# Second block's query, key and gate projections as seven block products of weight pairs, head norms with narrow sums

## The reference, cut to what matters

```python
hn = rms_norm(x, norm1_g[l])
proj = hn @ w_in[l]                      # 1024 x 5120
# qa, ka, va, qb, kb, vb: 8 heads of 64 each; gate_a, gate_b: 1024 wide each
out_a = chunked_attention(qa, ka, va, q_norm_g[l], k_norm_g[l], rel_bias[l])
out_b = stick_breaking_attention(qb, kb, vb)
mixed = (jax.nn.sigmoid(gate_a) * (out_a @ w_branch_a[l])
         + jax.nn.sigmoid(gate_b) * (out_b @ w_branch_b[l]))
x = x + mixed @ w_out[l]
```

## Time and profile before

| what | us |
| --- | --- |
| median of 3 runs (range) | 3571.55 (3569.49 to 3575.08) |
| the profiled execution, device time | 3567.36 |
| its span, first to last instruction | 3565.5 |
| PE busy | 3283.7 (92%) |
| DVE / ACT / POOL busy | 2166.0 / 1244.7 / 866.0 |
| mean granted clock of PE | 0.960 of full |

### The profile page before, as it was taken

How to read it: one execution, slowest core, us unless ns; L and a number is a source line. 1 busy time by engine, 2 the same in 40 slices (tenths; PEclk the granted TensorE clock), 3 DMA queues, 4 the chain that set the end, 5 groups by cost and what they waited for, 6 DMA issues and landing times.

```text
span 3565.5 us, 36894 instructions
## 1 busy us (share of the span) xinstructions
PE 3283.7 (92%) x14740; PEld 2553.0 (72%) x14740; DVE 2166.0 (61%) x2476; ACT 1244.7 (35%) x1843; POOL 866.0 (24%) x815
## 2 busy tenths in 40 slices
PE   6878998998798899999997999999889979999999
PEld 3657776666676678888886778865447767888787
DVE  5454445886676887775446571137763589888433
ACT  3332111554223433333334222137551344444322
POOL 1310210123333243331000100001653244333101
PEclk9889998999999999999999999999999999999999
DMA  3443344002344222225432434321104422222543
GB/s 141 142 148 112 106 173 148 21 22 72 129 136 137 94 95 83 83 76 175 130 123 94 142 123 121 95 73 54 36 20 142 154 71 89 83 77 77 191 128 124
DMA packets 107043, 377.98 MB, mean 106 GB/s; under 512 B 13783, under 2 KB 16471, under 8 KB 106488
## 3 DMA queue, kind: packets, MB, share of 16 engines
q1 hardware_dynamic: 61976, 217.79, 19.3%
q0 software_dynamic: 44896, 157.84, 12.5%
HBM read 296.93 MB, written 78.64 MB: 105 GB/s over the span
## 4 chain that ended last, share of the span: by engine, by line
PE 56%; DVE 10%; issue 6%; POOL 2%; ACT 2%; DMA 0%; POOLq 0%; DVEq 0%; ACTq 0%
PE PS L360 17%; PE PS L362 17%; PE PS L361 17%; DVE HL L317 1%; PE PS L2809 1%; DVE E L2941 1%; PE PS L2770 1%; PE PS L2792 1%; POOL Sc L3010 1%; DVE QR L1395 1%; DVE HTf L1665 0%; ACT HL L301 0%; DVE Rk L2621 0%; POOL HT L1831 0%; PE PS L2546 0%
## 5 line engine op out<-in xcount | busy, mean ns | idle before, releaser
L360 PE MATMUL PS<-H,HL 128*128 128x512 f32 x2176 | 874.3, 402 | 77.4 <-DVE HL L317 23.5
L362 PE MATMUL PS<-H,HL 128*128 128x512 f32 x2176 | 858.9, 395 | 0.0
L361 PE MATMUL PS<-H,HL 128*128 128x512 f32 x2176 | 857.6, 394 | 0.0
L317 DVE TENSOR_TENSOR HL<-RAW,HL 128x1024 fp32r<-128x1024 f32 (+1 forms) x412 | 480.9, 1168 | 617.1 <-ACT HL L301 612.9
L301 ACT ACTIVATE HL<-RAW 128x1024 fp32r<-128x1024 f32 (+1 forms) x412 | 368.8, 896 | 1203.6 <-PE PS L362 1111.2
L360 PEld LDWEIGHTS PS<-H,HL 128*128 128x128 f32 x2176 | 415.1, 191 | 182.0 <-DVE HL L317 32.9
L361 PEld LDWEIGHTS PS<-H,HL 128*128 128x128 f32 x2176 | 415.9, 191 | 91.6 <-issue 4.6
L362 PEld LDWEIGHTS PS<-H,HL 128*128 128x128 f32 x2176 | 414.9, 191 | 91.5
L360 PE MATMUL PS<-hsr,HL 128*128 128x512 f32 x704 | 278.4, 396 | 1.8 <-DVE rows L2096 1.8
L361 PE MATMUL PS<-hsr,HL 128*128 128x512 f32 x704 | 278.5, 396 | 0.0
L362 PE MATMUL PS<-hsr,HL 128*128 128x512 f32 x704 | 276.5, 393 | 0.0
(11 more groups left out here) (352 smaller groups left out, 5256.4 us busy)
## 6 DMA issues: line engine op xcount, KB each, us to landing
RAW<-in_w_up SPq DMA_DIRECT2D x98, 512.0 KB, 3.6
RAW<-in_w_down SPq DMA_DIRECT2D x88, 512.0 KB, 3.6
RAW<-in_w_proj SPq DMA_DIRECT2D x48, 512.0 KB, 4.3
scr_hid<-hidr POOLq DMA_DIRECT2D x36, 512.0 KB, 2.9
HTf<-scr_hid POOLq DMA_DIRECT2D x72, 256.0 KB, 3.7
RAW<-in_w_wmodr SPq DMA_DIRECT2D x32, 512.0 KB, 4.5
RAW<-in_w_wout SPq DMA_DIRECT2D x26, 512.0 KB, 3.8
RAW<-in_w_wmod SPq DMA_DIRECT2D x16, 512.0 KB, 4.1
```

Of the source, the lines that this page charges most:

```text
L317: e.tensor_tensor(lo, part_source(k, j, x)[0], hi.bitcast(F32), ALU.subtract).then_inc(*k.low.mark(j, x))
L360: e.matmul(out, lh, rh, start=first, stop=False)
L361: e.matmul(out, lh, rl, start=False, stop=False)
L362: return e.matmul(out, ll, rh, start=False, stop=last)
```

## The change

- **Projection.** The 32 units are run as 16 pairs, `P2`, normed pairs alternating with plain ones at first, each pair as seven products of 12 matrix instructions, in the feed-forward's scheme. The combinations t1 to t4 of H are formed by DVE and ACT during the values of half 1 (t1 after them, since it takes the place of a part of H). Values of half 1 now follow directly on those of half 0.
- **Middle.** The rows of half 1 are formed earlier (during value units 5 to 7 of half 0), in place instead of in a buffer `ot`; therefore the residual x is first stored to memory (`mid_store`), reloaded during the gate pairs, multiplied by its norm on DVE, and stored again.
- **Head norms.** Squares of a pair go to a tile `sqt`; 16 products of 128 tokens with columns of a selector `sel` (32 columns wide) leave the sums of the pair's 4 heads x 8 token blocks in 32 rows of 128. DVE and ACT work on these 32x128; the result is stored to memory (512 bytes a row) and read back four times 64-fold into `sqt`, which spreads each factor over its head's 64 rows; DVE then multiplies.
- **End.** The bias table and the first keys, values and queries lie where t2 to t4 lie now, so POOL loads them after m7 of the last pair, and the bias of heads 5 to 7 after its m4.

```diff
-    units("proj2", [*range(32, 40), *range(3), *range(32, 40), *range(3, 32)])
+    for _ in range(2):
+        units("proj2", range(32, 40))
+    for a, b in P2:
+        out.extend([("proj2", a, "first"), ("proj2", b, "full")])
...
+P2 = [(0, 1), (8, 9), (2, 3), (10, 11), (4, 5), (12, 13), (6, 7), (14, 15)] + [(n, n + 1) for n in range(16, 32, 2)]
...
-            if h == 0 and vs == 1 and u_ == 1:
+            if h == 0 and vs == 1 and u_ == 0:
                 free = mid_sum(k, e, F, free, 1)
...
@@ pe_proj2
+    def square_sums(i):
...
+        for a, n in enumerate(P2[i]):
+            e.wait_ge(*s.act.at("sq", n))
+            for t in range(8):
+                c = 8 * a + t
+                x = e.matmul(PS[0:32, 2, 0:128], k.sel[:, blk(c, 32)], k.sqt[:, a, blk(t)], start=c == 0, stop=c == 15)
...
+    free = pe_values(k, e, F, 0, free)
     free = pe_values(k, e, F, 1, free)
+    for i, (n0, n1) in enumerate(P2):
...
+        for x in PRODUCTS["full"]:
+            w, f, b = take_part(k, e, j, x), FACTOR[x], p2_bank(x, i)
+            claim(b)
+            for q in range(4):
+                e.wait_ge(*mid_block_ready(k, f, q))
+                hi, lo = block(k, f, q)
+                y = mm3(e, PS[:, b, :], w[0][:, blk(q)], w[1][:, blk(q)], hi, lo, q == 0, q == 3)
...
+            if normed(i - 1) and x == "m6":
+                square_sums(i - 1)
...
@@ pool_proj2
+    def load_factors(i):
+        e.wait_ge(*k.st_rq.at(i))
+        for a in range(2):
+            e.wait_ge(*s.pe.at("sq", i))
+            for hh in range(2):
+                to = k.sqt[64 * hh:64 * hh + 64, a, :].rearrange("p (t n) -> p t n", t=8)
+                c = 16 * a + hh
+                e.dma_start(to, k.d_rq[i // 2][c:c + 15:2].partition_broadcast(64)).then_inc(*k.in_rq[a].mark(i, hh))
...
+    e.wait_ge(*s.pe.at("m7", NP2 - 1))
+    load_queries(k, e, 0)
+    load_pair(k, e, 0)
+    e.dma_start(k.B[:, 0:5, :], k.A["bias2"][0:5].rearrange("h p n -> p h n")).then_inc(*k.in_bias[0].mark(0))
+    load_queries(k, e, 1)
+    load_pair(k, e, 1)
+    e.wait_ge(*s.pe.at("m4", NP2 - 1))
+    e.dma_start(k.B[:, 5:8, :], k.A["bias2"][5:8].rearrange("h p n -> p h n")).then_inc(*k.in_bias[1].mark(5))
+    e.wait_ge(*s.dve.at("x", 7, 1))
+    e.dma_start(k.d_x[7], k.xs[:, 1, :]).then_inc(*k.st_xs[1].mark(7))
+    store(NP2 - 1)
```

More of the change, by code:

```diff
@@ L2248, in pool_down @@
     for m in range(N_HALF, len(LOADED)):
+        if m == len(LOADED) // 2 + N_HALF and not F.second:
+            mid_store(k, e, F, 0)
         load_hidden(k, e, F, m)
-    if F.second:
+    if not F.second:
+        mid_store(k, e, F, 1)
+    else:
         for hf in range(2):
@@ L2490, in pool_mid_residual @@
[L2490 to L2494, removed]
[L2500 to L2506 removed]
+            mid_rows(k, e, 0, 1)
@@ L2538, in claim @@
             e.wait_ge(*x)
[L2540 to L2568, removed]
[L2569 to L2574 removed]
+    def square_sums(i):
+        e.wait_ge(*s.dve.at("sel", 2))
+        claim(2)
+        for a, n in enumerate(P2[i]):
[3 more added lines that the diff above has]
+                x = e.matmul(PS[0:32, 2, 0:128], k.sel[:, blk(c, 32)], k.sqt[:, a, blk(t)], start=c == 0, stop=c == 15)
+        x.then_inc(*s.pe.mark("sq", i))
+        free[2] = [s.dve.at("m", i)]
@@ new lines, in act_proj2 @@
+    for i in range(NP2):
+        if i:
+            finish(i - 1)
+        e.wait_ge(*s.pe.at("m1", i))
+        if i:
+            e.wait_ge(*s.dve.at("c11", i - 1))
+        e.activation(k.s1p[:, :], k.PS[:, p2_bank("m1", i), :], ACT.Copy).then_inc(*s.act.mark("s1", i))
+        by(i, "m1")
+        by(i, "m6")
+        by(i, "m5")
+        if normed(i - 1):
+            e.wait_ge(*s.dve.at("m", i - 1))
+            e.activation(k.rq[:, :], k.rq[:, :], ACT.Sqrt).then_inc(*s.act.mark("m", i - 1))
+        by(i, "m7")
+        by(i, "m2")
+        by(i, "m3")
+        by(i, "m4")
@@ new lines, in pool_proj2 @@
+    for i in range(NP2):
+        if i and not normed(i - 1):
+            store(i - 1)
+        if normed(i - 1):
+            e.wait_ge(*s.dve.at("inv", i - 1))
+            e.dma_start(k.d_rq[i // 2], k.rq[:, :]).then_inc(*k.st_rq.mark(i - 1))
+        for m in residual_rows(i - 1):
+            e.wait_ge(*s.dve.at("x", m, 1))
+            e.dma_start(k.d_x[m], k.xs[:, m % 2, :]).then_inc(*k.st_xs[m % 2].mark(m))
+            if m + 2 < 8:
+                load_x(m + 2)
+        if i + 2 < NP2:
+            pair_sums(k, e, p2_unit(k, i + 2))
+        if normed(i - 1):
+            load_factors(i - 1)
+        if normed(i - 2):
+            store(i - 2)
+        if i == NP2 - 8:
+            for n in P2[6]:
+                e.wait_ge(*s.dve.at("n", n))
+            for h in range(2):
+                e.wait_ge(*k.st_res[h].at(k.mid, 7))
+            load_x(0)
+            load_x(1)
@@ L3169, in pool_program @@
     pool_branch(k, e)
-    after(e, *k.branch.every())
+    after(e, *k.branch.every(), *k.st_xs)
     pool_halves(k, e, k.O2)
```

350 lines of the change are left out of this document (231 added, 119 removed).

## The result

The changed kernel takes **3523.8 us** (median of 4 runs, 3520.8 to 3529.0) against 3570.5 for the kernel before in runs beside it (4 runs, 3562.3 to 3575.1): a ratio of 0.9873, 95% interval 0.985 to 0.9896. The same kernel measured again later gave 3527.7 and 0.9891 (0.9877 to 0.9904). The forecast was 3526, in a range of 3511 to 3544.

The account below looks back on a forecast made before the run. PE, busy 92% of the span, was taken as the bound. Terms -39.1 - 9.7 - 6.3 + 2.0 + 0 + 7.4 = -45.7 us took the profiled 3567.36 to 3521.7; with 4.2 for the median, 3526 us, range 3511 to 3544.

Parts of the forecast that it names:

- Pairs: Projection: 16 pairs of 84 instructions at 19.32 us replace 32 units of 48 at 10.88 us; -39.1 us.
- First hole: PE's 13.23 us hole before half 1's values: rows start earlier, about 3.5 us of hole left; -9.7 us.
- Second hole: PE's 4.61 us wait for a weight split behind two head-norm inverses disappears, with its slow start; -6.3 us.
- New small wait: Before the first pair's m1, ACT's two splits and a copy make PE wait; +2.0 us.
- Square sums: Head norms: the new narrow products take 3.5 us a pair, 13.8 in all, as before; 0 us.
- Stage to T: Stage up to T, the end of its last matrix instruction: terms for pairs, holes, new wait and square sums; -53.1 us.
- End: Stage end: 7.6 MB of transfers land at T + 13, delaying the attention's first DVE step from T + 5.6; +7.4 us.
- (a): Stage end costs almost nothing, as transfers run side by side; with cheap square sums about 3517 us; chance 0.12.
- (b): First hole stays, as rows, high parts, splits and copies form one chain; 9.7 us worse, 3536 us; chance 0.10.
- (c): DVE becomes the bound in the scaling pairs; up to 6.4 us in each of four, 3552 us; chance 0.06.
- (d): Head-norm factors come back too late; 12 us lost in each of four pairs, 3574 us; chance 0.04.

Follow-up runs that it names:

- the doubled product: Changed kernel with product m7 of each of the 16 pairs computed twice, the first result dropped; 3568.9 us, ratio to the kernel before 1.000.
- One line in the kernel before: Kernel before, with the first three value units of a half taken one at a time, each with its part; 3559.6 us, ratio 0.998.
- the rows late again: Changed kernel with half 1's row steps and high parts back behind half 0's value copies; one run, hole 3.52 us, stage to T 406.1 us.
- copies-first run: Changed kernel with ACT's copies of the last value banks ahead of high parts 6 and 7 and of the splits; one run, 3521.7 us.
- lean versions: The lean run, 3514.5 us, and the same end combined with the copies-first run's edit, 3513.4 us and later 3509.9.
- order run: Changed kernel with the last residual row and last gates stored ahead of the bias of heads 5 to 7; 3529.5 us, ratio 0.9883.
- lean run: Changed kernel with pair 1's keys and values and bias of heads 2 to 7 loaded inside the attention, last sigmoids ahead of a split; 3514.5 us.
- run with late factors: Changed kernel with the factors' four spreading loads issued between the third and fourth weight sum of the next pair; one run, 3539.6 us.

## Why the prediction was right, point by point

- **Pairs, -39.1.** Right: 19.32 us a pair, PE full for 320 us, and the doubled product costs what its instructions cost.
- **First hole, -9.7.** It gave 13.23 + 1.73 - 2.27 - 1.64 = 11.05 us, with eight distances behind the wait taken for the slow start each time. The size was near, but the step was wrong in its cause. I read the hole as the rows of half 1 coming late and their earlier start as the gain. The row that releases it is not a row step but a weight split (`HL L317`); what stood in front of PE was the list that takes three units at once. One line in the kernel before gives 10.7 us; with the rows late again the changed kernel loses 1.3 at this place. The copy `ev` as the new releaser was foreseen; it came 1.2 us sooner than worked out.
- **Second hole, -6.3.** Gone as said.
- **New small wait, +2.0.** 1.81, at the ACT copies. The copies-first run took 1.0 of it away and moved the time as the mechanism asks.
- **Square sums, 0.** 3.61 a block, 14.4 in all, against 13.8: +0.6. The value between the two nearest rows held.
- **Stage to T.** The terms gave -53.1, the traces -54.1; most of the difference is the first hole.
- **End, +7.4.** This is the term that was mis-sized: +11.0. I had 7.6 MB at 390 to 400 GB/s, flowing from T - 6 and done at T + 13, with one or two weight units among them. 8.13 MB moved, since three weight units ran beside. In the 8 us before T it was 280 GB/s, 2.2 MB; the 5.9 MB left behind T went at 358 GB/s, which is 16.5 us. So about half of the miss lies in the bytes left behind T and half in the rate. The last gates could not be issued before T + 3.8 either, as ACT had a split, two small copies and two sigmoids in front of them, of which I had counted one step of 0.7; but the DMA engines were full meanwhile, and no run shows that this alone set the end. The Trainium skill (DMA: Bandwidth & Descriptors, Specifications) gives about 358 GB/s as a core's limit to HBM. The window of 16.6 us has the same figure; but two windows of the lean versions behind T show 371 and 372 over 7 us, and the earlier trace rows 390 over 2. By its figure the term had been +9.4, the nearer one.
- **What made the total fit.** The end cost 3.6 us more than forecast and the stage 1.0 less; 3.5 us less than before lie in stretches that the change doesn't touch. The forecast's 2 us of error are smaller than its parts' errors, which is partly luck.
- **Rivals.** (a), an end at almost no cost: the order run shows that issue order doesn't buy it, the lean run that fewer bytes, together with an earlier sigmoid, do. (b), the first hole stays: no. (c), DVE bound beside POOL's sums: the lengthening is there (below), but PE never waited in a scaling pair. (d), factors too late: they had 11.4 us to spare before PE, 6.5 before DVE.

## What to carry to other kernels

Read who releases a hole before pricing it, and look what PE had in hand at that moment: a wait placed ahead of work that doesn't need it costs as much as late work, and is one line to mend. Where loads wait for a space that the last products still use, load first only what the next stage's first units need, and put the large rest behind the landing that releases that stage, not merely behind its issue. Measure a stage between events that both versions have, since stretches that nobody touched moved by up to 10 us here; and look at the granted clock behind each small wait before a difference of 1 or 2 us is given to an edit.

## What the runs showed of the hardware that I had not expected

**The clock after a wait.** The four waits of PE in the run with late factors are nearly alike, 2.98 to 3.29 us, and stand at the same point of a pair. Two were followed by the lower level, two were not. Behind the second, instructions start 0.43 apart from 0.8 us on; the first window, with the first wait, has a granted clock of 1.00, the one with the second 0.72 (columns as in the earlier trace rows):

```profile
2104.35 0.47 PE L365 MATMUL PS<-HT,HL 128*128 128x512 f32 x1 [3.29 <-DVE ev L2776]
...
2105.15 0.63 PE L365 MATMUL PS<-HT,HL 128*128 128x512 f32 x1
2105.57 0.63 PE L366 MATMUL PS<-HT,HL 128*128 128x512 f32 x1
```

```profile
2056.00:2062.00 6.00, 3.62 (x19) 2.87 (x20) 5.22 (x7) 2.40 (x3) 0.69 (x1) 1.00 0.26 47
2103.00:2109.00 6.00, 4.65 (x14) 3.45 (x15) 4.47 (x7) 3.12 (x4) 1.72 (x2) 0.72 0.28 85
```

In the changed kernel the wait of 2.27 us was followed by the lower level and that of 1.81 was not; with the rows late the same wait, 1.82 long, was. The last early wait of the values was 2.37 us in the changed kernel and 2.39 in the copies-first run, and only the second was followed by it. So the length of one wait doesn't tell which level follows, and a small wait has two prices: by itself, or with some 1.6 us behind it.

**DVE beside POOL.** In the changed kernel's scaling pairs, DVE steps that lie beside POOL's weight sums take up to 2.6 times as long, and POOL's steps too. DVE and POOL in time (start, us, instruction):

```profile
2045.49 1.28 DVE L2735 SCALAR_TENSOR_TENSOR ev<-ev,lamb,sqt 128x1024 f32<-128x1024 f32 x1
2046.68 1.78 DVE L320 TENSOR_TENSOR HL<-RAW,HL 128x512 fp32r<-128x512 f32 x1
2048.39 0.68 DVE L2774 TENSOR_TENSOR ev<-PS,u4p 128x512 f32<-128x512 f32 x1
2048.99 1.71 DVE L2735 SCALAR_TENSOR_TENSOR ev<-ev,lamb,sqt 128x1024 f32<-128x1024 f32 x1
```

```profile
2045.74 2.17 POOL L253 TENSOR_TENSOR SX<-RAW 128x512 f32<-128x512 f32 x1 [8.10 <-DMA RAW<-in_w_proj]
```

The split is 1.78 where it takes 0.67 to 0.69 alone, the first sum 2.17 where it takes 1.30. The step at 2048.39, which reads one operand from PSUM, keeps its 0.68. The Trainium skill (SBUF — State Buffer, SBUF: two separate sides) says that of a DVE step with two SBUF inputs and a GpSimd step the one that starts first holds a shared port pair for its whole length, and the other waits. The rows agree: POOL's sum starts 0.25 us after the first DVE step and takes 0.9 us longer than alone, where 1.0 of that step was left, and the split behind it ends about 0.6 us after POOL's sum, near its own length. The cost stays on DVE and POOL; PE's windows are full there.
